# Attention pairs: inverse softmax sums made 64 wide by VectorE and transposed, instead of spread by products with the identity

## The reference

```
s = einsum('bqhd,bkhd->bhqk', q, k) * scale        # 256 x 256 logits of a head
s = where(allowed, s, -inf)                        # causal, or top-k keys, or none
p = softmax(s, axis=-1)
o = einsum('bhqk,bkhd->bqhd', p, v)                # 64 wide per head
```

## Time and profile before

| | |
|---|---|
| median of 3 runs | 2849.75 us |
| profiled execution | 2847.14 us |
| its span | 2845.2 us |
| TensorE busy (matmul) | 2540.8 us, 89% |
| TensorE weight loads | 1641.6 us, 58% |
| VectorE busy | 1273.5 us, 45% |
| ScalarE busy | 382.3 us, 13% |
| GpSimd busy | 211.9 us, 7% |
| DMA | 703.57 MB, mean 247 GB/s |

### The profile page before, as it was taken

One profiled execution on the slowest core, in us unless ns is written; L12 is line 12 of the kernel. 1 busy time (PEld: TensorE's weight loads), 2 busy tenths in 40 slices (PEclk: granted clock), 3 DMA queues, 4 the chain that ended last, 5 costly groups with the idle time before them and its releaser, 6 DMA issues.

```text
span 2845.2 us, 37997 instructions
## 1 busy us (share of the span) xinstructions
PE 2540.8 (89%) x16098; PEld 1641.6 (58%) x16098; DVE 1273.5 (45%) x2575; ACT 382.3 (13%) x847; POOL 211.9 (7%) x224
## 2 busy tenths in 40 slices
PE   9999999999999999999999999867667999766765
PEld 5779755896669947699457785322223675222221
DVE  4866644665466666877557543000002553000102
ACT  1410002100131001310022111000000412000000
POOL 0300012000120000400003000000000310000000
PEclk9999999999999999999999999987888999877887
DMA  8354543544535435254431858999999457999998
GB/s 320 119 162 159 183 137 126 192 162 150 192 103 179 177 118 200 91 191 164 148 122 56 292 222 337 421 422 421 421 421 388 181 188 281 421 422 421 421 421 341
DMA packets 245772, 703.57 MB, mean 247 GB/s; under 512 B 18795, under 2 KB 123753, under 8 KB 197219
## 3 DMA queue, kind: packets, MB, share of 16 engines
q1 hardware_dynamic: 244304, 699.30, 65.0%
q10 hardware_dynamic: 1299, 1.83, 0.2%
HBM read 698.20 MB, written 1.05 MB: 246 GB/s over the span
## 4 chain that ended last, share of the span: by engine, by line
PE 73%; DMA 20%; SPq 4%; DVE 2%; ACT 1%; issue 1%; DVEq 0%; ACTq 0%
PE lin L909 47%; PE sco L909 15%; PE trp L909 9%; DMA ring<-in_moe_w_up 8%; DMA ring<-in_moe_w_gate 5%; SPq L741 3%; DMA ring<-in_moe_w_down 3%; PE trp L1078 1%; DMA x<-in_moe_w_down 1%; DMA arena<-in_moe_w_down 1%; DMA spare<-in_moe_w_up 1%; PE trp L1174 1%; SPq L746 0%; SPq L743 0%; ACT arena L2303 0%
## 5 line engine op out<-in xcount | busy, mean ns | idle before, releaser
L909 PE MATMUL lin<-ring,arena 128*128 128x512 f32 (+4 forms) x2260 | 773.5, 537 | 17.7 <-DMA ring<-in_moe_w_down 7.1
L909 PEld LDWEIGHTS lin<-ring,arena 128*128 128x128 f32 (+1 forms) x2260 | 367.7, 176 | 341.7 <-issue 317.6
L909 PE MATMUL sco<-ring,arena 128*32 128x512 f32 (+2 forms) x1340 | 337.9, 800 | 159.8 <-DMA ring<-in_moe_w_up 54.4
L909 PE MATMUL lin<-arena 128*128 128x128 f32 (+9 forms) x3312 | 453.8, 347 | 21.7 <-DMA ring<-in_moe_w_down 7.7
L909 PE MATMUL sco<-arena 128*32 128x512 f32 (+6 forms) x1888 | 412.1, 469 | 54.4 <-DMA ring<-in_moe_w_gate 24.6
L3715 DVE TENSOR_TENSOR arena<-arena,sco 128x512 f32<-128x512 f32 x16 | 11.0, 688 | 759.7 <-PE sco L909 759.7
L909 PEld LDWEIGHTS lin<-arena 128*128 128x128 f32 (+4 forms) x3312 | 288.5, 161 | 100.6 <-issue 80.6
L909 PEld LDWEIGHTS sco<-ring,arena 128*32 128x32 f32 (+1 forms) x1340 | 89.6, 149 | 328.7 <-issue 326.5
L909 PEld LDWEIGHTS sco<-arena 128*32 128x32 f32 (+3 forms) x1888 | 160.1, 160 | 153.3 <-issue 145.7
L909 PE MATMUL trp<-arena 128*128 128x128 f32 (+2 forms) x1584 | 217.7, 292 | 1.1 <-ACT arena L2488 0.7
L2776 POOL TENSOR_TENSOR roots<-roots 128x1 f32<-128x1 f32 (+2 forms) x42 | 38.9, 927 | 2283.6 <-DVE roots L2898 2261.1
(11 more groups left out here) (367 smaller groups left out, 2390.6 us busy)
## 6 DMA issues: line engine op xcount, KB each, us to landing
ring<-in_w_gate_up SPq DMA_DIRECT2D x88, 1024.0 KB, 5.7
ring<-in_moe_w_up SPq DMA_DIRECT2D x82, 1024.0 KB, 26.7
ring<-in_moe_w_gate SPq DMA_DIRECT2D x75, 1024.0 KB, 27.0
arena<-in_moe_w_down SPq DMA_DIRECT2D x56, 1024.0 KB, 27.0
ring<-in_moe_w_down SPq DMA_DIRECT2D x51, 1024.0 KB, 26.7
ring<-in_w_down SPq DMA_DIRECT2D x44, 1024.0 KB, 5.3
arena<-in_moe_w_gate SPq DMA_DIRECT2D x44, 1024.0 KB, 26.9
arena<-in_moe_w_up SPq DMA_DIRECT2D x34, 1024.0 KB, 27.0
```

What stands on the lines that cost most here:

```text
L909: return nc.tensor.matmul(o, lhsT, rhs, start=start, stop=stop, skip_group_check=not one_group)
```

## The change

In place of the products with the identity, VectorE writes the inverses out in SBUF as a 128 x 256 array, `wide`: for each tile of 128 queries, 64 copies of the first head's inverse and 64 of the second's. TensorE transposes its two 128x128 halves into the same place of the PSUM bank. On VectorE the reciprocal now stands ahead of `second_turned(i)`, and the new copy, `widen(i)`, between `second_turned(i)` and `maxima(i+2)`. On TensorE the transposes of pair i-1 stand ahead of `turn(i)`, where `spread_inverses` stood between logits(i+2) and the value products; for the last pair they stand directly ahead of its value products. The waits on `pair_stored` and, for a stage's first pair, on `proj_done` and `banks_free` move with them. Units of layer 1 keep `spread_inverses`. One scratch array of the latent layer, `head_sums`, moves to another address to make room.

```diff
             if kind == LATENT:
-                late = [at(ATT + 5120, 3, P), at(PROJ + 2048, 3, P)]
+                late = [at(PROJ + 2432, 3, P), at(PROJ + 2048, 3, P)]
...
+        def wide_inverses(kind):
+
+            return at(PROJ + 1152 if kind == 0 else ATT + 5376, NT, 2, 64)
...
-                def values(i):
+                def turn_inverses(i):
                     j = base + i
-                    _, v, causal_pair = pairs[i]
-                    for done in pair_PT_done:
-                        pe.wait_ge(done, j + 1)
                     if j >= 2:
                         pe.wait_ge(pair_stored, j - 1)
                     if i == 0:
                         pe.wait_ge(proj_done, t_proj.n + 2)
                         if banks_free is not None:
                             banks_free()
+                    pe.wait_ge(pair_widened, j + 1)
+                    for t in range(NT):
+                        nc.tensor.transpose(lin[:, 2 + j % 2, SEQ + t * P:SEQ + (t + 1) * P],
+                                            wide[:, t, :, :].rearrange("p e d -> p (e d)"), ident[:, :])
+
+                def values(i):
+                    j = base + i
+                    _, v, causal_pair = pairs[i]
+                    if i == count - 1:
+                        turn_inverses(i)
+                    for done in pair_PT_done:
+                        pe.wait_ge(done, j + 1)
                     bank = lin[:, 2 + j % 2, :]
-                    pe.wait_ge(pair_inverted, j + 1)
-                    spread_inverses(bank[:, SEQ:2 * SEQ], pair_rinv[:, j % 2, :])
...
                 for i in range(count):
+                    if i > 0:
+                        turn_inverses(i - 1)
                     turn(i)
                     if i + 2 < count:
                         logits(i + 2)
...
+                def widen(i):
+                    j = base + i
+                    dve.wait_ge(pair_inverted, j + 1)
+                    inverses = pair_rinv[:, j % 2, :].rearrange("p (e t) -> p t e", e=2)
+                    V.tensor_copy(wide[:, :, :, :], inverses.unsqueeze(3).to_broadcast([P, NT, 2, 64])).then_inc(pair_widened, 1)
...
                 for i in range(count):
+                    invert(i)
                     second_turned(i)
+                    widen(i)
                     if i + 2 < count:
                         maxima(i + 2)
-                    invert(i)
                     if i > 0:
                         store(i - 1)
```

More of the change, by code:

```diff
@@ L472, in build @@
         pair_inverted, unit_inverted = sem("pair_inverted"), sem("unit_inverted")
+        pair_widened = sem("pair_widened")
         pair_summed, pair_stored = sem("pair_summed"), sem("pair_stored")
@@ L1142, in spread_inverses, with attend_pairs @@
                 return last
-            def attend_pairs(pairs, between=None, behind_logits=None, banks_free=None, behind_turns=None):
+            def attend_pairs(wide, pairs, between=None, behind_logits=None, banks_free=None, behind_turns=None):
                 base, count = pairs_done[0], len(pairs)
@@ L1781, in mla @@
                                   [[mla_v[:, k, 64 * (2 * b + e):64 * (2 * b + e) + 64] for k in range(NT)] for e in range(2)], True))
-                first, last_values = attend_pairs(pairs)
+                first, last_values = attend_pairs(wide_inverses(LATENT), pairs)
                 output_products(LATENT, [[(pair_stored, first + 2 * u + 2)] for u in range(4)], last_values, (pair_logits, first + 1))
@@ L2219, in _ @@
                     pe.wait_ge(unit_masked, len(UNIT_ITEMS))
-                    first, last_values = attend_pairs(mem_pairs, behind_logits=lambda: unit_values(0, lin[:, 2:4, :], proj),
+                    first, last_values = attend_pairs(wide_inverses(kind), mem_pairs, behind_logits=lambda: unit_values(0, lin[:, 2:4, :], proj),
                                                       banks_free=lambda: pe.wait_ge(unit_stored, 1), behind_turns=lambda: turn_unit(1))
@@ L2226, in _ @@
                 else:
-                    first, last_values = attend_pairs(mem_pairs + pairs, last_chunk)
+                    first, last_values = attend_pairs(wide_inverses(kind), mem_pairs + pairs, last_chunk)
                     output_products(kind, [[(pair_stored, first + 2 * u + 2)] for u in range(4)], last_values,
@@ L3009, in store_unit, with attend_pairs @@
                 dve.wait_ge(unit_stored, u + 1)
-            def attend_pairs(masks, blocks, between=None):
+            def attend_pairs(wide, masks, blocks, between=None):
                 base, count = pairs_done[0], len(masks)
@@ L3597, in mla @@
                 t_proj.skip(2 + 2 + 2)
-                attend_pairs([causal] * (MLA_HEADS // 2), range(KD))
+                attend_pairs(wide_inverses(LATENT), [causal] * (MLA_HEADS // 2), range(KD))
             def route(layer):
@@ L3927, in _ @@
                 if kind != 1:
-                    attend_pairs(mem_masks + [dsa_mask if kind == 0 else causal] * (HEADS // 2), mem_blocks + list(range(HEADS // 2)),
+                    attend_pairs(wide_inverses(kind), mem_masks + [dsa_mask if kind == 0 else causal] * (HEADS // 2), mem_blocks + list(range(HEADS // 2)),
                                  last_keys if kind == 0 else None)
@@ L3932, in _ @@
                     mask_units(ring[:, s, 0:3 * NT * SEQ].rearrange("p (g t k) -> p g t k", g=3, t=NT))
-                    attend_pairs(mem_masks, mem_blocks, lambda: store_unit(0, lin[:, 2:4, :]))
+                    attend_pairs(wide_inverses(kind), mem_masks, mem_blocks, lambda: store_unit(0, lin[:, 2:4, :]))
                     store_unit(1, sco[:, :, :])
```

## The result

The changed kernel takes 2856.41 us (median of 10 runs, 2854.28 to 2859.47) against 2849.72 us for the kernel before (10 runs). The ratio is 1.0023, with a 95% interval of 1.0015 to 1.0031: slower by 6.7 us. The prediction said 2857.5, from +7.8 us. The profiled execution took 2856.08 us with a span of 2854.0, 8.8 us more than before.

What follows compares the result with a forecast made beforehand. TensorE bounded the pairs at 2.90 us, VectorE close behind. Layers 0 and 3 at +3.85 each, layer 2 +1.4, layer 1 0, latent -1.3 gave +7.8 us: 2854.9 profiled, 2857.5 median; range 2847 to 2864.

Steps and rivals of the forecast that it cites:

- The copy is held by GpSimd: VectorE's widening copy waits for GpSimd's running instruction to end and finishes 0.15 us later; unheld it takes 0.30 us.
- How often it is held: Layers 0, 2, 3: three long GpSimd operations pass per pair, so widenings under them wait; stages +3.85, +1.4, +3.85 us.
- the price of one hold: Under GpSimd operations of 1.27 us, a pair costs 3.85 us in place of 2.90, +0.95.
- the short operations: GpSimd operations of 0.46 us: the copy waits 0.1 to 0.4 us, about +0.2 to +0.3 a pair.
- VectorE becomes the bound: In causal pairs the bound moves from TensorE, then wanting 2.73 us a pair, to VectorE at 3.01.
- its work per pair: VectorE's work in a causal pair: 2.71 us plus 0.30 for the widening copy, 3.01.
- +0.11 a steady pair: Causal pair without a hold: 3.01 us on VectorE against 2.90 before.
- Rival 3: Faster: TensorE's order still sets the pair, the copy hides in VectorE's 0.19 us gap; -5.8 us, 2844; chance 0.08.
- The added wait decides nothing: TensorE's wait on `pair_widened` ahead of turns: about 2.1 us to the next widening, costing only in layers 1 and 0's first pairs.
- Layer 1: 0: Layer 1's two pairs: waiting for the first widening and dropping 0.38 us of spreading balance; 0, between -0.2 and +0.6.
- The latent layer: VectorE's 3.01 us stays under TensorE's 3.38, early waits go into idle time; 8 x 0.17 saved, -1.3 us.
- One for one to the end: A delay of TensorE in attention isn't made up afterwards and reaches the end of the kernel in full.

Runs made afterwards that it cites:

- kept_busy: Changed kernel plus four unread products per stage beginning with memory pairs, ahead of TensorE's first wait for the widened inverses: 2852.97 us, ratio 1.0011.
- quiet_after: Changed kernel with GpSimd's sums of weight rows cut from 512 to 8 columns: 9115.81 us, unusable as a total; only first-block stages were read.
- quiet_before: Kernel before with GpSimd's sums of weight rows cut from 512 to 8 columns: 9101.61 us, unusable as a total; only first-block stages were read.
- late_turn: Changed kernel with the inverses' transposes back directly ahead of the value products and two arrays of widened inverses in turn: 2851.69 us, ratio 1.0006.
- act_late: Changed kernel with the widening as a copy on ScalarE, transposes directly ahead of the value products, two arrays: 2851.96 us, ratio 1.0006.
- psum_late: Changed kernel with small inverses in PSUM as the widening copy's source, transposes directly ahead of the value products, two arrays: 2844.49 us, ratio 0.9982.

## Why the prediction was right, and where only its sum was

**The copy is held by GpSimd: right, and shown** three ways: by the copies' own times, by the quiet pair, and by the copy from PSUM that never waits. Its price is kept_busy against before, less quiet_after against quiet_before, all at clock 1.00: layer 0 +1.97 - (-0.63) = 2.60 us, layer 3 +1.93 - (-0.62) = 2.55, layer 2 +0.26 - (-1.39) = 1.65. Together 6.8 us. The unread products of kept_busy may be part of it: with late_turn in its place the three are 2.20, 2.20 and 1.16, together 5.6.

**How often it is held: mis-sized; the price of one hold: right.** A pair with a long hold takes 3.86 to 3.89 us at clock 1.00, as forecast (3.85). But I let every steady pair under long operations pay, because VectorE would come 0.3 us after the start of GpSimd's third operation. It comes at that very start, in layer 0 once 0.03 us ahead and once 0.04 us behind, and a few hundredths decide. Layer 0 has two long holds (1.33 and 1.37 us) with a free copy between them, layer 3 two in a row, layer 2 one and one of 1.01; kept_busy and late_turn have two in a row in layer 0. And the short operations, for which I booked 0.2 to 0.3 us a pair, held no copy of layers 0, 2 and 3. The forecast had some 10 us for the holds in these layers.

**VectorE becomes the bound: right; its work per pair: mis-sized.** 2.77 us, not 2.71 + 0.30. The widening's price was taken at the duration of the nearest operation, 0.29, rounded up; start to start it is 0.20, and the copy out of `trp` ahead of it hands over after 0.46 us. So what I booked as +0.11 a steady pair is a gain of 0.13, and with the ends the change is worth 0.6 to 1.4 us a stage when nothing holds it. Rival 3 had this sign; it named VectorE's 0.19 us gap as the point from which it decides, and the addition to VectorE's chain came out at 0.06.

**The added wait decides nothing: wrong.** The step said that the wait on `pair_widened` costs only what was counted in the first pairs. It left out the clock. TensorE idles 2.60 us at it in layers 0 and 3 and then runs at half clock; the changed kernel against kept_busy puts this at 1.22 + 2.66 = 3.9 us in layers 0 and 3 of one execution each. Between medians it is 3.4 us, and the two intervals of the ratio overlap, so the size is less certain than the cause. "Layer 1: 0" failed for another reason: 1.64 of its 2.24 us are missing in kept_busy, where the clock held, and in this execution it had fallen ahead of the wait. It falls there without the change as well.

**The latent layer: right**, -1.27 against -1.3, at 3.34 us a pair.

**One for one to the end: right** within the first block, where 0.1 us came between stages. That the span is longer by +8.8 with +8.87 in the stages is in part luck, since the differences around the latent layer cancel.

So the measured sum is: holds +6.8, gains of the unheld pairs -2.6, clock of layers 0 and 3 +3.9, layer 1 +2.2, latent layer -1.3, and -0.1 of layer 2 between the changed kernel and kept_busy, +8.9 in all. Too much for the holds, about 3 us in layers 0, 2 and 3, and 1.6 us too little gain in the unheld pairs, stood against a clock that wasn't in the sum. The total is close because errors of both signs met, and it should not be taken as proof of its terms.

Left open: why one of act_late's two equal waits of 2.21 us brought the clock down and the other did not, and how often it falls in layer 1 of either kernel; the profiles are one execution each.

## What to carry to other kernels

Before an SBUF-to-SBUF copy is given to VectorE, look at what GpSimd does in that stage: a 0.28 us copy cost up to 1.37 us, and with its source in PSUM it cost 0.41 always. A wait put early in TensorE's order costs more than its own length if the clock falls behind it; put the new operation directly ahead of its reader. psum_late did both, and turned +6.7 us into -5.3. Look at the clock of the stage before the wait, too: in layer 1 it had fallen already. And price an added VectorE operation by distances between starts, on a kernel bounded by two engines at once.

## What the runs showed of the hardware that I had not expected

A float32 reciprocal on VectorE takes 1.74 us for 256 elements and 0.17 us for 4, so 6.2 ns for each further element, against 0.41 us for a copy of 256 from PSUM. And 0.07 us between the starts of a copy and a GpSimd operation (0.03 ahead, 0.04 behind) decides between 0.28 and 1.37 us. The granted clock fell behind idle times of 2.21 to 3.71 us in seven of eight cases in layers 0 and 3, in the changed kernel's layer 0 only after about 1.4 us of further work; it stayed at 1.00 behind 1.54 us and less in all twenty others.

The Trainium skill (SBUF — State Buffer, "Who interferes with whom") says that issue order, not the operation's shape, decides who blocks; the trace agrees, with those two copies. It also says that an instruction with at most one SBUF input outside the two-port modes does not contend; the 34 copies from PSUM agree (409 to 417 ns). The 34 reciprocals (1741 to 1744 ns) fit as well, though no run shows which mode they use.
